# Summing the modulation columns with TensorE matmuls in four column groups instead of VectorE passes

## The chip, the cores and the metric

The kernel runs on one NeuronCore of a Trainium2 chip. The time is device microseconds of one execution; the median of several executions is compared, kernel against kernel on the same chip. The core's engines are TensorE (PE, with its weight loads shown as PEld), VectorE (DVE), ScalarE (ACT), GpSimd (POOL) and the queue of DMA issues on SyncE (SP). They run side by side and wait for each other by semaphores.

## The reference: what is computed

One inference step of a two-layer trunk on 128 context and 1,024 latent tokens, 1,152 in all, with 1,024 channels. Layer 0 mixes tokens by a bidirectional retention and a chunked gating MLP, layer 1 by a bidirectional gated linear recurrence; each is followed by a squared-ReLU MLP of width 4,096. Each sub-layer is normalized and modulated by a shift, a scale and a gate that come from a conditioning vector, one for the context and one for the latents:

```python
for l in range(DEPTH):                       # DEPTH = 2
    mod = (silu(cond) @ mod_w[l] + mod_b[l])[:, None, :]   # mod_w[l]: 1024 x 6144
    sh1, sc1, g1, sh2, sc2, g2 = jnp.split(mod, 6, axis=-1)
    h = rmsnorm(x, norm_mix[l]) * (1.0 + sc1) + sh1
    mix = token_mixing[l](h)                 # retention and gating MLP, or recurrence
    x = x + g1 * mix
    h = rmsnorm(x, norm_mlp[l]) * (1.0 + sc2) + sh2
    ff = jnp.square(jax.nn.relu(h @ mlp_w1[l])) @ mlp_w2[l]
    x = x + g2 * ff
```

The change concerns the first line: the product of two conditioning vectors (context and latents) with the modulation weights, 96 columns of 128 channels over both layers. All arithmetic is at float32 precision.

## The kernel before

**Layout.** Activations lie with channels on the 128 partitions and the 1,152 tokens along them, in eight tiles `x[:, k, :]`. A projection of 1,024 inputs to 128 outputs is a *unit*: `project` calls `three_passes` (the matmuls of L800), eight tiles by three products (high by high, high by low, low by high parts of input and weight) by three banks of 384 tokens, 72 matmuls. Results go to one of two sets of three PSUM banks, taken in turn by `take_set`; the reader gives a set back by `read_out`. GpSimd splits each unit's weights into high and low parts (L689, L691), SyncE loads them two units ahead (`load_unit`, L519).

**Stages.** First, tokens are turned into columns, and the scale and shift columns of layer 0 are made (16 of the 96) with whole rows of `mod_w` as the moving operand: `row_half` (L896) holds 32 conditioning columns `cond_wide` (two real, 30 zero) as weights in four column groups of the array and streams 512 columns of weights past each, and `first_columns` (L903) turns the sums back into columns. Then layer 0: four *heads*, each with six units and ten small stages (*minis*: transposes with `turn`, L832, and 128x128 products) interleaved in an order written out by hand; `out_proj`; the first MLP, eight *groups* of four units in and four units out (`mlp`). Then layer 1 and its MLP, which have no modulation columns to make. Each engine has a program of its own, with loops of the same shape (`head`, `group`).

**Modulation columns before.** The other 80 columns are made one at a time, eight in each head and six in each group of the first MLP, in the background of the work that they are for. SyncE's `load_mod` (L521 to L527) brings the 1,024 x 128 weights of a column in two halves to `mod_raw`, a single buffer: a half is loaded once the sum of the column before has read it (`mod_summed`). VectorE's `sum_mod` (L1724 to L1750) multiplies the eight 128x128 tiles by the conditioning value of their row and adds them up, for the two conditioning vectors, 16 passes in two dependent chains (L1734, L1739), into `mod_sum`. TensorE's `mod_column` (L821 to L828) then sums over the partitions: two matmuls with `mod_sum` as weights and one column of ones (L827) into `mod_psum`. `mods_out` (L1721) adds the bias and puts a batch of columns into `mod`, from which later steps take shifts, scales and gates.

**Order around it.** In a head TensorE's order is unit 0, the column left over from the head before, unit 1, column 0, a mini, unit 2, column 1, and so on (`mod_col`). VectorE does the sum of column n between the same stages (`next_mod`), and SyncE issues column m behind the weights of a unit as `mods_behind` says. In the MLP, columns follow the units (`mod_col(j - 1)`, `mod_col(3)`, `mod_col(2 + j)`). In the first head the rope tables, the first column, weights and the two cached states are issued one after another on SyncE, while ScalarE issues a spill of all of x to memory (`spill`, L1493).

Of the kernel before, what the change touches and what calls it, by code (L numbers as in the profile page):

```python
# [33 lines left out]
P = 128  # L34
# [137 lines left out]
def build(nc, a):  # L172
    with ExitStack() as ctx:
# [31 lines left out]
        mod_sum = sb("mod_sum", [2, 2, P])  # L205
# [78 lines left out]
        row_sum = sb("row_sum", [NCH])  # L284
        mod = sb("mod", [2, MODS, 2])
# [21 lines left out]
        mod_psum = banks[:, 2 * BANKS, 512 - 4 * MODS:512]  # L307
        ssq_psum = banks[:, 2 * BANKS + 1, :]
# [19 lines left out]
        mod_summed = sem("mod_summed")  # L328
        mod_used = sem("mod_used")
# [451 lines left out]
        def _(pe):  # L781
# [39 lines left out]
            def mod_column(i, per, c):  # L821

                pe.wait_ge(mod_summed, at(i, 2 * per, 2 * (c - FIRST_MODS) + 4))
                start = at(i, 2 * per, 2 * c)
                for n in range(2):
                    dst = mod_psum[:, start + n:start + n + 1] if isinstance(start, int) else mod_psum[:, ds(start + n, 1)]
                    last = pe.matmul(dst, mod_sum[:, c % 2, n, :], ones[:, 0:1], start=True, stop=True)  # L827
                last.then_inc(mod_used, 1)  # L828
# [97 lines left out]
            def head(h):  # L926
# [37 lines left out]
                def mod_col(c):  # L964
                    if c == 0:
                        pe.wait_ge(mod_read, h + FIRST_BATCHES)
                    mod_column(h, HEAD_MODS, M0 + c)

                big(0, 0).then_inc(unit_done, 1)
                if not first_head(h):  # L970
                    mod_column(h, HEAD_MODS, M0 - 1)
                big(1, 1).then_inc(unit_done, 1)
                mod_col(0)
# [4 lines left out]
                mod_col(1)  # L978
# [3 lines left out]
                mod_col(2)  # L982
                big(5, 3).then_inc(unit_done, 1)
                mod_col(3)
# [12 lines left out]
                last.then_inc(mini_done, 1)  # L997
                big(9, 4).then_inc(unit_done, 1)
                mod_col(4)
# [12 lines left out]
                mod_col(5)  # L1012
# [4 lines left out]
                mod_col(6)  # L1017
# [35 lines left out]
            def mlp(l):  # L1053
                I, U = AT_MLP[l].items, AT_MLP[l].units

                def group(g):
                    def mod_col(c):
                        if l == 0:
                            if c == 0:
                                pe.wait_ge(mod_read, g + (FIRST_BATCHES + HEADS))  # L1060
                            mod_column(g, GRP_MODS, MODS + c)
# [581 lines left out]
        def _(dve):  # L1643
# [28 lines left out]
            dve.tensor_copy(ident[:], consts[:, C_ID:C_ID + P])  # L1672
            dve.tensor_copy(q_rows[:].rearrange("p d t -> p (d t)"), consts[:, C_QF:C_QF + 2 * P])
# [50 lines left out]
            def sum_mod(i, per, c):  # L1724

                dve.wait_ge(mod_used, at(i, per, c - 1))
                for half in range(2):
                    dve.wait_ge(mod_landed[half], at(i, 16 * per, 16 * (c - FIRST_MODS + 1)))
                    for k in range(KT // 2):
                        for n in range(2):  # L1730
                            w, total = mod_raw[:, half, k, :], mod_sum[:, c % 2, n, :]
                            s = cond[:, n, half * KT // 2 + k:half * KT // 2 + k + 1]
                            if half + k == 0:
                                op = dve.tensor_scalar(total, w, s, None, ALU.mult)  # L1734
                                op.then_inc(dve_step, 1)
                                done = steps.done()
                            else:
                                after(chain[n])
                                op = dve.scalar_tensor_tensor(out=total, in0=w, scalar=s, in1=total, op0=ALU.mult, op1=ALU.add)  # L1739
                                if k == KT // 2 - 1 and n == 1:  # L1740
                                    op.then_inc(mod_summed, 1)
                                    done = None
                                else:
                                    op.then_inc(dve_step, 1)
                                    done = steps.done()
                            chain[n] = done
                    if half == 0:

                        dve.wait_ge(mod_summed, at(i, 2 * per, 2 * (c - FIRST_MODS) + 3))
                        chain[1] = chain[0]  # L1750

            chain = [None, None]
# [82 lines left out]
            def mlp(l):  # L1835
# [3 lines left out]
                def group(g, last):  # L1839
                    if l == 0:  # L1840
                        steps.enter(None if last else g, 14 * GRP_MODS)
                    for j in range(GRP):
# [19 lines left out]
                        if l == 0:  # L1862
                            sum_mod(g, GRP_MODS, MODS + j)
                    for k in range(2 * GRP):
                        s = (I + GRP + k) % 2
                        if k % 2 == 0:
                            dve.wait_ge(mini_done, at(g, GRP_MINIS, M + k // 2 + 1))
                        else:
                            dve.wait_ge(unit_done, at(g, GRP_UNITS, U + GRP + k // 2 + 1))
                        update(s, k, l, G2).then_inc(read_out[s], 1)  # L1870
                        if l == 0 and k in (1, 3):
                            sum_mod(g, GRP_MODS, MODS + GRP + k // 2)
                        if last and k and l == 0:
                            low_part(k - 1, gained(norm, k - 1)[:], H_NORM[norm], k - 1)
                        if last and k > 1:
                            add_square(norm, k - 1)
                        if last and k == 0 and l == 0:
                            gains_early()
                    if l == 0:
                        steps.leave(1 if last else GROUPS - 1)  # L1880
                        mods_out(1, g * GRP_MODS, GRP_MODS, at(g, GRP_MODS, MODS + GRP_MODS))
# [193 lines left out]
            def head(h, last_head):  # L2075
                steps.enter(None if isinstance(h, int) else h, 41 + 14 * HEAD_MODS)
# [7 lines left out]
                def next_mod(n):  # L2084
                    sum_mod(h, HEAD_MODS, FIRST_MODS + n)
# [31 lines left out]
                scale_out(s, 1, v_raw).then_inc(read_out[s], 1)  # L2117
                mini(0)
# [5 lines left out]
                next_mod(1)  # L2124
                next_mod(2)
# [4 lines left out]
                next_mod(3)  # L2130
# [10 lines left out]
                scale_out(s, 3, v_raw).then_inc(read_out[s], 1)  # L2141
                mini(2)
# [271 lines left out]
```

## Time and profile before

| | |
|---|---|
| Median of 3 runs | 2621.42 us (2617.94 to 2622.23) |
| The profiled execution | 2624.58 us, span 2622.4 us |
| TensorE busy | 2534.9 us, 97% of the span |
| VectorE busy | 1791.2 us, 68% |
| ScalarE / GpSimd busy | 803.9 us / 794.3 us |
| Mean DMA rate | 73 GB/s |
| Modulation sums on VectorE (L1734, L1739) | 160 and 1,120 instructions, 82.8 and 337.6 us |
| Column matmuls on TensorE (L827) | 320 records, 41.0 us |

Busy times are sums of what an engine was at work on; matmuls are pipelined, so that neighbours overlap, and a matmul's recorded duration is longer than the time until the next one starts. The stages lie at these times of the span: first columns to 65 us, the four heads from there to 469 us, the output projection to 562 us, the first MLP with its norm to some 1,403 us, layer 1 behind it.

### The profile page before, as it was taken

Reading aid. Unit: us, or ns where it says so; the run is one execution under the profiler, and the core shown is the slowest. Engines: PE = TensorE matmul, PEld = TensorE weight load, DVE = VectorE, ACT = ScalarE, POOL = GpSimd, SP = SyncE. Lnnn points to the kernel's source line nnn. Section 1 sums busy time; section 2 is a strip of 40 time slices with the busy share of each in tenths; the row PEclk is TensorE's granted clock in tenths of the full one; section 3 lists DMA queues with packets and bytes.
Section 4 is the critical chain, followed back from the end, with each engine's and each line's share of the span. In section 5 each row is a group of like instructions: output and inputs, shape, how many; then the busy total and the mean of one; then the engine's idle time right before and its main releaser. Section 6 shows DMA issues by size and latency. Waiting matters only on the chain.

```text
span 2622.4 us, 42028 instructions
## 1 busy us (share of the span) xinstructions
PE 2534.9 (97%) x15122; PEld 2476.8 (94%) x15122; DVE 1791.2 (68%) x3174; ACT 803.9 (31%) x1271; POOL 794.3 (30%) x575
## 2 busy tenths in 40 slices
PE   8999999999999999999999999799999999999998
PEld 6999999899999999999998888598999999999987
DVE  5888778568567576585588988836756556656664
ACT  5333223132102112011035666703323432432323
POOL 1221221322222222222222221122445445535521
PEclk8999999999999999999999999899999999999999
DMA  6422222312222222222222111222111011111131
GB/s 247 157 74 75 73 76 67 129 49 81 65 73 72 64 78 66 64 88 60 76 80 102 39 40 40 63 78 96 50 48 48 32 48 48 40 40 56 32 121 73
DMA packets 261367, 190.71 MB, mean 73 GB/s; under 512 B 9253, under 2 KB 253733, under 8 KB 260262
## 3 DMA queue, kind: packets, MB, share of 16 engines
q1 hardware_dynamic: 260004, 174.71, 21.8%
q10 hardware_dynamic: 1282, 14.93, 1.4%
q8 instruction: 50, 0.82, 0.1%
q14 instruction: 31, 0.25, 0.0%
HBM read 170.20 MB, written 19.41 MB: 72 GB/s over the span
## 4 chain that ended last, share of the span: by engine, by line
PE 78%; DVE 14%; issue 4%; ACT 2%; DMA 1%; SPq 0%; DVEq 0%; POOL 0%; ACTq 0%; POOLq 0%
PE psum L800 61%; PE psum L1131 12%; DVE mod_sum L1739 2%; PE psum L1182 2%; DVE gated_f L2308 1%; PE psum L827 1%; DVE h_lo L1772 1%; DVE sumsq L1710 1%; DVE x L1796 1%; DMA mod_raw<-in_mod_w 1%; DVE sumsq L1781 1%; DVE h_lo L1765 1%; DMA x_spill<-x 1%; DVE x L1968 0%; DVE mod_sum L1734 0%
## 5 line engine op out<-in xcount | busy, mean ns | idle before, releaser
L800 PE MATMUL psum<-h_hi,w_hi 128*128 128x384 f32 (+1 forms) x2880 | 674.1, 342 | 23.2 <-DVE gate_raw L1791 9.5
L800 PE MATMUL psum<-h_lo,w_hi 128*128 128x384 f32 (+1 forms) x2880 | 660.6, 338 | 0.0
L800 PE MATMUL psum<-h_hi,w_lo 128*128 128x384 f32 (+1 forms) x2880 | 660.0, 337 | 0.0
L800 PEld LDWEIGHTS psum<-h_hi,w_hi 128*128 128x128 f32 x2880 | 514.8, 189 | 36.9 <-issue 9.9
L689 POOL CAST w_hi<-w_raw 128x1024 fp32r<-128x1024 f32 x120 | 132.9, 1108 | 1321.6 <-PE psum L800 786.1
L800 PEld LDWEIGHTS psum<-h_lo,w_hi 128*128 128x128 f32 x2880 | 519.7, 189 | 0.0
L800 PEld LDWEIGHTS psum<-h_hi,w_lo 128*128 128x128 f32 x2880 | 518.3, 189 | 0.0
L1739 DVE SCALAR_TENSOR_TENSOR mod_sum<-mod_raw,cond,mod_sum 128x128 f32<-128x128 f32 x1120 | 337.6, 371 | 9.8 <-DMA mod_raw<-in_mod_w 2.2
L1796 DVE SCALAR_TENSOR_TENSOR x<-psum,mod,x 128x768 f32<-128x768 f32 (+2 forms) x264 | 145.9, 611 | 244.3 <-PE psum L800 244.3
L691 POOL TENSOR_TENSOR w_lo<-w_raw,w_hi 128x1024 fp32r<-128x1024 f32 x120 | 289.5, 2412 | 9.6
L1955 DVE TENSOR_TENSOR x<-x,psum 128x576 f32<-128x576 f32 x280 | 203.7, 752 | 103.1 <-PE psum L1131 102.5
L1319 ACT ACTIVATE relu<-relu,bias 128x384 f32<-128x384 f32 x64 | 36.0, 609 | 612.3 <-DVE relu L1851 612.3
L800 PE MATMUL psum<-hid_hi,w_hi 128*128 128x384 f32 x864 | 199.6, 338 | 7.3 <-DVE raw L1906 6.3
L800 PE MATMUL psum<-hid_lo,w_hi 128*128 128x384 f32 x864 | 196.7, 335 | 0.0
L800 PE MATMUL psum<-hid_hi,w_lo 128*128 128x384 f32 x864 | 196.5, 335 | 0.0
L1131 PE MATMUL psum<-b_hi,w_hi 128*128 128x288 f32 x784 | 168.1, 296 | 2.9 <-DVE raw L1906 2.0
L1131 PE MATMUL psum<-b_lo,w_hi 128*128 128x288 f32 x784 | 167.9, 296 | 0.0
L1131 PE MATMUL psum<-b_hi,w_lo 128*128 128x288 f32 x784 | 167.9, 296 | 0.0
L800 PEld LDWEIGHTS psum<-hid_hi,w_hi 128*128 128x128 f32 x864 | 153.1, 189 | 8.4 <-DVE raw L1906 6.6
L800 PEld LDWEIGHTS psum<-hid_lo,w_hi 128*128 128x128 f32 x864 | 154.7, 188 | 0.0
L800 PEld LDWEIGHTS psum<-hid_hi,w_lo 128*128 128x128 f32 x864 | 154.4, 188 | 0.0
L1131 PEld LDWEIGHTS psum<-b_hi,w_hi 128*128 128x128 f32 x784 | 126.6, 189 | 3.3 <-DVE raw L1906 2.2
(279 smaller groups left out, 3090.3 us busy)
## 6 DMA issues: line engine op xcount, KB each, us to landing
w_raw<-in_mlp_w SPq DMA_DIRECT2D x128, 512.0 KB, 4.1
mod_raw<-in_mod_w SPq DMA_DIRECT2D x160, 256.0 KB, 2.9
x_spill<-x ACTq DMA_DIRECT2D x3, 4608.0 KB, 14.5
w_raw<-in_ab_w_in SPq DMA_DIRECT2D x24, 512.0 KB, 4.3
w_raw<-in_lru_w_in SPq DMA_DIRECT2D x16, 512.0 KB, 4.2
x<-x_spill SPq DMA_DIRECT2D x2, 2880.0 KB, 9.6
x_old<-x_spill SPq DMA_DIRECT2D x8, 576.0 KB, 6.3
x_rows<-in_x_sample SPq DMA_DIRECT2D x8, 512.0 KB, 6.8
```

The lines of the kernel that those rows point to most:

```text
L689: pool.tensor_copy(w_hi[:, s, :], w_raw[:, s, :]).then_inc(hi_done, 1)
L691: pool.tensor_tensor(w_lo[:, s, :], w_raw[:, s, :], w_hi[:, s, :].bitcast(F32), ALU.subtract).then_inc(split_done, 1)
L800: mm = pe.matmul(psum[:, s, c, 0:end - c * CH], w, v[:, k, c * CH:end], start=(first and n == 0 and w is hi[k] and v is in_hi), stop=(last ...
L827: last = pe.matmul(dst, mod_sum[:, c % 2, n, :], ones[:, 0:1], start=True, stop=True)
L1131: mm = pe.matmul(banks[:, pair + b, 0:HB], w, v[:, p, hb, b * HB:(b + 1) * HB], start=(p == 0 and m == 0), stop=(p == 1 and m == 2))
L1182: last_mm = pe.matmul(psum[:, s, c, 0:CH], gate_w[:, 2 * d + kind, :], xc[:, c * CH:(c + 1) * CH], start=True, stop=True)
L1319: act.activation(relu[:, t], relu[:, t], ACT.Relu, bias=bias[:, j, 0:1]).then_inc(relu_ready, 1)
L1710: dve.tensor_tensor(sumsq[:], sumsq[:], square(n, k)[:], ALU.add).then_inc(sq_added, 1)
L1739: op = dve.scalar_tensor_tensor(out=total, in0=w, scalar=s, in1=total, op0=ALU.mult, op1=ALU.add)
L1765: dve.tensor_tensor(h_lo[:, k, 0:width], of, h_hi[:, k, 0:width].bitcast(F32), ALU.subtract).then_inc(h_ready, 1)
L1796: last = dve.scalar_tensor_tensor(out=dst, in0=src, scalar=mod[:, l, gate + k, c:c + 1], in1=dst, op0=ALU.mult, op1=ALU.add)
L1955: last = dve.tensor_tensor(t, t, banks[:, pair:pair + 2, 0:HB], op)
```

## The change

The sum over the 1,024 rows is made by TensorE alone, in the way the first 16 columns are made, 128 columns at a time. `mod_burst` waits for a half of `mod_raw` and does four matmuls, one in each column group, with the conditioning columns of a tile (`cond_wide`, 128x32) as weights and the 128x128 tile of `mod_raw` as moving operand; the second half adds to the same sums in `row_psum`, a part of the bank that holds `mod_psum`. VectorE's `row_out` copies the 128x128 result to `mod_row`. `mod_column` does one matmul with `mod_row` as weights and `pick` (two columns that pick and add the four groups' rows of each conditioning vector) as moving operand, and gives both values of the column. The 16 VectorE passes and their chains go away. A half of `mod_raw` is now free when TensorE's burst has read it (`mod_summed` comes from TensorE).

Column and burst stand together (`mods`): behind a unit, TensorE does the matmul of the column before and then the burst of the next. The column that stood between a mini and unit 3, and the one behind unit 3, move to other places, as do VectorE's `next_mod` calls. DMA issues stay as they are.

```diff
             def mod_column(i, per, c):
 
-                pe.wait_ge(mod_summed, at(i, 2 * per, 2 * (c - FIRST_MODS) + 4))
+                pe.wait_ge(row_copied, at(i, per, c - FIRST_MODS + 1))
                 start = at(i, 2 * per, 2 * c)
-                for n in range(2):
-                    dst = mod_psum[:, start + n:start + n + 1] if isinstance(start, int) else mod_psum[:, ds(start + n, 1)]
-                    last = pe.matmul(dst, mod_sum[:, c % 2, n, :], ones[:, 0:1], start=True, stop=True)
-                last.then_inc(mod_used, 1)
+                dst = mod_psum[:, start:start + 2] if isinstance(start, int) else mod_psum[:, ds(start, 2)]
+                pe.matmul(dst, mod_row[:, c % 2, 0, :], pick[:], start=True, stop=True).then_inc(mod_used, 1)
+
+            def mod_burst(i, per, c):
+
+                for half in range(2):
+                    pe.wait_ge(mod_landed[half], at(i, 16 * per, 16 * (c - FIRST_MODS + 1)))
+                    for q in range(KT // 2):
+                        last = pe.matmul(row_psum[WIDE * q:WIDE * (q + 1), :], cond_wide[:, half * KT // 2 + q, :], mod_raw[:, half, q, :],
+                                         start=(half == 0), stop=(half == 1))
+                    last.then_inc(mod_summed, 1)
...
-                def mod_col(c):
-                    if c == 0:
+                def mods(column, burst):
+
+                    if column == 0:
                         pe.wait_ge(mod_read, h + FIRST_BATCHES)
-                    mod_column(h, HEAD_MODS, M0 + c)
+                    if column >= 0 or not first_head(h):
+                        mod_column(h, HEAD_MODS, M0 + column)
+                    mod_burst(h, HEAD_MODS, M0 + burst)
 
                 big(0, 0).then_inc(unit_done, 1)
-                if not first_head(h):
-                    mod_column(h, HEAD_MODS, M0 - 1)
+                mods(-1, 0)
                 big(1, 1).then_inc(unit_done, 1)
-                mod_col(0)
+                mods(0, 1)
...
                 big(3, 2).then_inc(unit_done, 1)
-                mod_col(1)
+                mods(1, 2)
                 s = mini(4)
                 pe.wait_ge(activated, at(h, HEAD_UNITS, 2))
                 turn(s, v_raw).then_inc(mini_done, 1)
-                mod_col(2)
                 big(5, 3).then_inc(unit_done, 1)
-                mod_col(3)
+                mods(2, 3)
...
+                mods(3, 4)
                 big(9, 4).then_inc(unit_done, 1)
-                mod_col(4)
+                mods(4, 5)
...
-                mod_col(5)
+                mods(5, 6)
...
                 big(13, 5, heads_passed if isinstance(h, int) and h == HEADS - 1 else None).then_inc(unit_done, 1)
-                mod_col(6)
+                mods(6, 7)
...
                         project(g, GRP_ITEMS, I + j, GRP_UNITS, U + j, *waits).then_inc(unit_done, 1)
-                        if j:
-                            mod_col(j - 1)
+                        mods(j - 1, j)
...
-                    mod_col(3)
+                    mods(3, 4)
...
                         if j > 1:
-                            mod_col(2 + j)
+                            mods(2 + j, 3 + j)
...
-            def sum_mod(i, per, c):
-
+            def row_out(i, per, c):
+
+                dve.wait_ge(mod_summed, at(i, 2 * per, 2 * (c - FIRST_MODS) + 4))
                 dve.wait_ge(mod_used, at(i, per, c - 1))
...
+                dve.tensor_copy(mod_row[:, c % 2, 0, :], row_psum).then_inc(row_copied, 1)
```

In VectorE's program `next_mod` and the MLP's `sum_mod` call `row_out`; in a head the copies of columns 1, 2 and 3 stand behind the scaling of units 1, 2 and 3.

## Rows read from the trace of the kernel before

**Rows 1.** The page: its chain by engine, and one of the costliest groups.

```profile
PE 78%; DVE 14%; issue 4%; ACT 2%; DMA 1%; SPq 0%; DVEq 0%; POOL 0%; ACTq 0%; POOLq 0%
...
L1739 DVE SCALAR_TENSOR_TENSOR mod_sum<-mod_raw,cond,mod_sum 128x128 f32<-128x128 f32 x1120 | 337.6, 371 | 9.8 <-DMA mod_raw<-in_mod_w 2.2
```

**Rows 2.** Windows: stretch and its length, busy us of each engine, clock, DMA.

```profile
core 0: us, PE busy (x) PEld busy (x) DVE busy (x) ACT busy (x) POOL busy (x), PEclk, DMA share, GB/s
706.00:1324.00 618.00, 618.00 (x3604) 617.89 (x3602) 402.62 (x966) 78.75 (x168) 165.15 (x96) 1.00 0.24 71
```

**Rows 3.** Timeline of TensorE in the first MLP: start, duration, instructions merged.

```profile
641.90 0.50 PE L827 MATMUL psum<-ones,mod_sum 128*128 128x1 f32 x4
642.26 0.79 PE L800 MATMUL psum<-hid_hi,w_hi 128*128 128x384 f32 x3
642.89 0.68 PE L800 MATMUL psum<-hid_lo,w_hi 128*128 128x384 f32 x3
```

**Rows 4.** Timeline around the shift rows, matmuls in four column groups.

```profile
51.51 0.69 PE L800 MATMUL psum<-h_hi,w_lo 128*128 128x384 f32 x3
52.12 0.16 PEld L896 LDWEIGHTS psum<-shift_raw,cond_wide 128*32 128x32 f32 x8 [0.25 <-issue]
52.12 3.64 PE L896 MATMUL psum<-shift_raw,cond_wide 128*32 128x512 f32 x32
52.58 0.13 PEld L896 LDWEIGHTS psum<-shift_raw,cond_wide 128*32 128x32 f32 x4 [0.30 <-issue]
53.01 0.13 PEld L896 LDWEIGHTS psum<-shift_raw,cond_wide 128*32 128x32 f32 x4 [0.30 <-issue]
...
55.70 0.80 PE L800 MATMUL psum<-h_hi,w_hi 128*128 128x384 f32 x3
...
56.33 0.68 PE L800 MATMUL psum<-h_lo,w_hi 128*128 128x384 f32 x3
```

**Rows 5.** The chain that ended last: start, us on the chain, what.

```profile
214.05 2.13 PE psum L987 x18
...
667.83 12.59 PE psum L800 x72
```

**Rows 6.** Waits of TensorE: waiting line, releaser, us in all, times, longest.

```profile
PE psum L827 <- DVE mod_sum L1739: 7.4, 8, 2.0
...
PE psum L800 <- DVE probs L2212: 1.3, 1, 1.3
...
PE psum L800 <- DVE x L1796: 1.0, 3, 0.4
```

**Rows 7.** Timeline of TensorE, first and last head; idle before in brackets.

```profile
97.71 0.81 PE L800 MATMUL psum<-h_hi,w_hi 128*128 128x384 f32 x3 [0.73 <-DVE turned L1791]
...
111.95 0.50 PE L827 MATMUL psum<-ones,mod_sum 128*128 128x1 f32 x4
...
465.84 3.19 PE L1024 MATMUL psum<-wsT,kT 128*128 128x128 f32 x18 [3.49 <-DVE k_fwd L1791]
```

**Rows 8.** Windows of 2 us behind two idle times; PEclk before DMA share.

```profile
98.00:100.00 2.00, 2.00 (x9) 2.00 (x9) 2.00 (x3) 1.97 (x3) 1.67 (x1) 0.59 1.04 311
...
468.00:470.00 2.00, 2.00 (x9) 2.00 (x9) 2.00 (x1) 1.44 (x2) 2.00 (x1) 0.50 0.00 0
```

**Rows 9.** Timeline of TensorE: the first matmuls of unit 1, first head.

```profile
65.29 0.98 PE L800 MATMUL psum<-h_hi,w_hi 128*128 128x384 f32 x3
```

**Rows 10.** Line L527 in two stretches: issues, first and last; landing.

```profile
L527 SPq DMA_DIRECT2D mod_raw<-in_mod_w x2: 378/410/441, 61.4 to 61.8; - x2
...
DMA to landing us min/median/max: 5.4/5.9/6.3
...
L527 SPq DMA_DIRECT2D mod_raw<-in_mod_w x2: 379/379/379, 69.9 to 75.2; - x2
...
DMA to landing us min/median/max: 9.2/11.4/13.7
```

**Rows 11.** DMA issues from 55 to 100 us: KB, median us to landing.

```profile
x_spill<-x ACTq DMA_DIRECT2D x1, 4608.0 KB, 16.9
```

More of the change, by code:

```diff
@@ L204, in build @@
         mod_raw = sb("mod_raw", [2, KT // 2, P], mod_raw_at)
-        mod_sum = sb("mod_sum", [2, 2, P])
+        mod_row = sb("mod_row", [2, 2, P])
         t_at = [region(TB) for _ in range(10)]
@@ L284, in build @@
         row_sum = sb("row_sum", [NCH])
+        pick = sb("pick", [2])
         mod = sb("mod", [2, MODS, 2])
@@ L307, in build @@
         mod_psum = banks[:, 2 * BANKS, 512 - 4 * MODS:512]
+        row_psum = banks[:, 2 * BANKS, 0:P]
         ssq_psum = banks[:, 2 * BANKS + 1, :]
@@ L328, in build @@
         mod_summed = sem("mod_summed")
+        row_copied = sem("row_copied")
         mod_used = sem("mod_used")
@@ L1056, in group, with mods @@
                 def group(g):
-                    def mod_col(c):
+                    def mods(column, burst):
                         if l == 0:
-                            if c == 0:
+                            if burst == 0:
                                 pe.wait_ge(mod_read, g + (FIRST_BATCHES + HEADS))
-                            mod_column(g, GRP_MODS, MODS + c)
+                            if column >= 0:
+                                mod_column(g, GRP_MODS, MODS + column)
+                            if burst < GRP_MODS:
+                                mod_burst(g, GRP_MODS, MODS + burst)
                     for j in range(GRP):
@@ L1672, in _ @@
             dve.tensor_copy(ident[:], consts[:, C_ID:C_ID + P])
+            dve.tensor_copy(pick[:], consts[:, C_SEL:C_SEL + 2])
             dve.tensor_copy(q_rows[:].rearrange("p d t -> p (d t)"), consts[:, C_QF:C_QF + 2 * P])
@@ L1722, in mods_out @@
                                   ALU.add).then_inc(mod_read, 1)
-            def sum_mod(i, per, c):
+            def row_out(i, per, c):
+                dve.wait_ge(mod_summed, at(i, 2 * per, 2 * (c - FIRST_MODS) + 4))
                 dve.wait_ge(mod_used, at(i, per, c - 1))
[L1727 to L1752, printed above, removed]
+                dve.tensor_copy(mod_row[:, c % 2, 0, :], row_psum).then_inc(row_copied, 1)
             def gains(n, batches):
@@ L1839, in group @@
                 def group(g, last):
-                    if l == 0:
-                        steps.enter(None if last else g, 14 * GRP_MODS)
                     for j in range(GRP):
@@ L1862, in group @@
                         if l == 0:
-                            sum_mod(g, GRP_MODS, MODS + j)
+                            row_out(g, GRP_MODS, MODS + j)
                     for k in range(2 * GRP):
@@ L1870, in group @@
                         update(s, k, l, G2).then_inc(read_out[s], 1)
-                        if l == 0 and k in (1, 3):
-                            sum_mod(g, GRP_MODS, MODS + GRP + k // 2)
+                        if l == 0 and k in (1, 5):
+                            row_out(g, GRP_MODS, MODS + GRP + k // 4)
                         if last and k and l == 0:
@@ L1879, in group @@
                     if l == 0:
-                        steps.leave(1 if last else GROUPS - 1)
                         mods_out(1, g * GRP_MODS, GRP_MODS, at(g, GRP_MODS, MODS + GRP_MODS))
@@ L2075, in head @@
             def head(h, last_head):
-                steps.enter(None if isinstance(h, int) else h, 41 + 14 * HEAD_MODS)
+                steps.enter(None if isinstance(h, int) else h, 41)
                 def unit(n):
@@ L2084, in next_mod @@
                 def next_mod(n):
-                    sum_mod(h, HEAD_MODS, FIRST_MODS + n)
+                    row_out(h, HEAD_MODS, FIRST_MODS + n)
                 def rotate(dst):
@@ L2117, in head @@
                 scale_out(s, 1, v_raw).then_inc(read_out[s], 1)
+                next_mod(1)
                 mini(0)
@@ L2123, in head @@
                 dve.tensor_scalar(by_bank(k_bwd[:]), whole(s), col(k_dec[:, 1, :], h), None, ALU.mult).then_inc(read_out[s], 1)
-                next_mod(1)
-                next_mod(2)
                 unit(2)
@@ L2129, in head @@
                 scale_out(s, 2, turned).then_inc(read_out[s], 1)
-                next_mod(3)
+                next_mod(2)
                 dve.wait_ge(projected, h * 2 + 2)
@@ L2141, in head @@
                 scale_out(s, 3, v_raw).then_inc(read_out[s], 1)
+                next_mod(3)
                 mini(2)
```

## The prediction

> **What bounds the kernel now.** I read the page first, then the windows by stage, then TensorE's timeline at the places that the diff touches, then its waits, and last the DMA rows of the first head. On the page the chain that ended last is TensorE for 78% and VectorE for 14%, and VectorE's largest removed group is 1,120 instructions of the modulation sums, 337.6 us [rows 1]. That looks like a large prize. The windows correct it: in six of the eight groups of the first MLP TensorE is busy for 618.00 of 618.00 us, while VectorE is busy for 402.62 [rows 2]. So in most of the stretch with modulation columns VectorE's time is hidden behind TensorE, and the profiled execution is 2622.4 us of span with 2.2 us around it. What the change takes off VectorE counts only where TensorE waits; what it gives TensorE counts nearly everywhere. The waits of TensorE on the sums are 7.4 us in 8 places [rows 6].
>
> **The columns on TensorE, old and new.** There are 80 columns: 4 heads of 8 and 8 groups of 6. A column now is two matmuls, four records. In the MLP they hold TensorE from 641.90 to 642.26, 0.36 us, and the next three matmuls take 0.63 us (642.26 to 642.89) [rows 3] where three of 72 in 12.59 us take 0.52 [rows 5]: 0.10 more, so a column costs 0.46 us. The new column is one matmul of the same shape with two columns instead of one. It should leave two records of 0.09 us, 0.18 us in all (below: it can't go under one record, 0.09; above: it costs what two do, 0.36).
>
> **The burst.** Each column gets eight new matmuls, two in each of four column groups, 128 columns long. Their like stands in the trace before: the shift rows, 16 matmuls of 512 columns on the same conditioning weights in the same four groups, 32 records [rows 4]. Their weight loads come in fours, at 52.58 and 53.01: a round of four takes 0.43 us, so four groups do run side by side. A quarter of the columns should take a quarter of that, 0.107 us, and a lone 128-column record in another place takes 2.13/18 = 0.118 [rows 5]. A burst is two matmuls deep, two records each: four rounds, 0.43 us. But the shift rows hold TensorE longer than their rounds. The three matmuls before would have ended at 51.51 + 0.52 = 52.03; the next begin at 55.70 and take 0.63 to 56.33, 0.11 too long. From 52.03 to 55.81 is 3.78 us, eight rounds are 3.41, so going into column groups and out again costs 0.37 [rows 4]. A burst is then 0.80 us.
> The Trainium skill (TensorEngine Tiling, Key Properties) says that changing the tiling mode drains TensorE. Every burst would pay that twice; the trace agrees, with 0.37 us for both, and a sum that left it out would be 80 x 0.37 = 30 us lower.
> Net per column: 0.18 + 0.80 - 0.46 = +0.52 us, 80 times is **+41.6 us**. It lies on the path wherever TensorE has no gap, which is all of the MLP. Below: no switch, +0.15 each, 12 us. Above: nothing side by side and each record at the 0.09 of today's short ones, 16 x 0.09 + 0.37 + 0.18 - 0.46 = +1.53, 122 us. I take the value of the shift rows, the same kind of matmul.
>
> **What VectorE gives back.** The waits on the sums, 7.4 us [rows 6], end: a copy of 128x128 in place of 16 passes of 371 ns [rows 1] is behind the burst by much less than the unit that follows. Their places are columns 2 and 5 of the first head, 5 and 6 of the later ones and one in the first MLP. Behind column 2 of the first head comes a wait of 0.73 us for the scaled unit, late because the sums stood ahead of it, and then unit 3 takes 97.71 to 111.95 = 14.24 us instead of 12.59 [rows 5, 7]: the granted clock, which had been full, is 0.59 in a stretch of 2 us after these two idle times, so mostly at 1.2 GHz, the lower of its two levels [rows 8]. That is 0.73 + 1.65. In the last head the last unit's scaling on VectorE stands behind the sums: TensorE idles 3.49 us, its next 18 records take 3.19 instead of 2.13 [rows 5, 7], and in the 2 us after that the clock is 0.50, that is 1.2 GHz, which costs another 1.0 [rows 8]. Then it waits 1.3 us for the masked sums `probs`, behind column 7's sum [rows 6]. Together 6.9. At the end of the MLP, waits of 1.0 us on the update of x stand behind two sums [rows 6]; I count them all. Sum: 7.4 + 2.4 + 6.9 + 1.0 = **-17.7 us**. Below: only the 7.4. Above: 20, with some short waits on other buffers that the bursts cover. The 80 copies cost nothing on the path: VectorE is idle for a third of the MLP [rows 2]. Uncovered they would be at most a pass each, 80 x 0.37 = 30 us.
>
> **What is late next.** The burst waits for the weights on TensorE itself, where before VectorE waited and TensorE went on. Behind the waiting instruction stand the next projection and so all later units. In the first head this bites twice. Unit 1 starts at 65.29 now [rows 9]. In the new order burst 0 stands before it, and column 0's halves are issued at 61.4 and 61.8 and land 5.4 and 6.3 us later, the second at 68.1 [rows 10]. That is 2.8 us of idle, less little: 2.7. Then column 1's load can go only after burst 0. Now it is issued at 69.9 and 75.2 and lands 13.7 and 9.2 us later, at 83.6 and 84.4 [rows 10], because it shares the engines with the 4.6 MB spill of x, 16.9 us [rows 11]. It will be issued some 3 us sooner but lie in the same queue behind that spill, so I take the same landing. TensorE ends unit 1 at about 68.6 + 12.6 = 81.2 and wants it then: 2.7 us once the burst's own time is taken off. I charge each stall one lowering of the clock, as behind the two idle times above, 1.6 us. Sum **+8.6 us**; below 2.7 (column 1 lands sooner, no lowering), above 12.
> From column 2 on a load goes when the burst before has read, and has a 12.6 us unit until the next. Bursts 4 and 6 of a head are closer, with only the short stages between (some 7 us), against 5.4 to 6.3 for a load even in the first head's traffic [rows 10]: nothing. SP's later loads stand behind these; they wait for TensorE instead of VectorE and go no later, so projection weights stay early.
>
> **Rivals.** (A) The forecast: 41.6 + 8.6 - 17.7 = +32.5 us. (B) It doesn't get slower: the switch of groups hides under the neighbours, so a column's net is +0.15 and the bill 12 us against 17.7 given back. For it: the chain gives VectorE 14% [rows 1]. Against it: the 0.37 is there in the only burst of this kind. It gives 2621 + 12 + 3 - 18 to 2621 + 12 + 9 - 18, that is 2618 to 2624; it decides if burst and column together take about 0.6 us (today's 0.46 and 0.15), where A has 0.98. (C) Short records don't run side by side: each is bound by its own start, 0.09 us as in today's columns [rows 3], and the bill is 122 us: 2621 + 122 + 9 - 18 = 2734. Against it: the eight first weight loads of the shift rows come within 0.16 us [rows 4].
> The Trainium skill (TensorEngine Tiling, Instruction Overhead) gives each matmul about 60 cycles; at 2.4 GHz that is 25 ns, an estimate, and 16 of them 0.40 us a burst: 32 us more if it adds up, nothing if the groups' streams cover it. The shift rows are too long to show it.
> (D) Loads come late in every head, not the first alone: bursts 4 and 6 wait. If such a load took the 9.2 us of the busy stretch [rows 10] it would be 2 to 3 us late, 8 times, 16 to 24 us: about 2674. Against it: no such traffic after the first head.
>
> **How the numbers follow.** A 0.74, B 0.12, C 0.07, D 0.07. The profiled execution, 2624.6 us, lies 3.2 above the median of the three timed runs; from the median, 2621.4 + 32.5 = 2654. A's own bounds: a switch dearer or cheaper by a third (80 x 0.12 = 10 us), stalls 3 to 12, gains 10 to 20 give 2636 to 2676. The range reaches on to 2630 and 2684, which takes D in and leaves out C and most of B. Within 0.2% is about what a measurement of this kernel can tell from no change, 5 us. A, C and D are slower; half of B is within, a little of it faster: faster 0.05, same 0.07, slower 0.88.
>
> **What would show it.** In the MLP: the group of eight units grows from 103.0 us by 6 x 0.52 = 3.1; bursts of 16 records over about 0.4 us and a gap of 0.2 to 0.3 us behind them. If the gap is missing, B; if a burst spans 1.4 us or more, C. In the first head: TensorE idle on a load of the modulation weights near 65 and 81 us. In later heads: no wait on modulation at all (else D). In the last head: no idle ahead of the group mixing, and no lowered clock. The forecast is wrong if a burst's whole price is not between 0.6 and 1.0 us.

## The result, and the profile after

The changed kernel takes **2641.5 us** (median of 4 runs, 2638.5 to 2642.4) against 2621.8 for the kernel before on the same chip (4 runs, 2617.9 to 2625.9). The ratio is 1.0073, 95% interval 1.0055 to 1.0090: some 20 us slower, where 32.5 were forecast. The profiled executions have spans of 2639.0 us after and 2622.4 before, 16.6 us apart.

On the page, the busy shares and the chain by engine answer to [rows 1]:

```profile
PE 2562.5 (97%) x16242; PEld 2488.4 (94%) x16242; DVE 1406.7 (53%) x1975; ACT 803.9 (30%) x1271; POOL 793.1 (30%) x575
...
PE 84%; DVE 8%; issue 3%; ACT 2%; DMA 1%; SPq 0%; DVEq 0%; POOL 0%; ACTq 0%; POOLq 0%
```

VectorE's share of the chain fell from 14% to 8%, and TensorE's rose from 78% to 84%. The window over the six groups of the first MLP in which TensorE never rests answers to [rows 2]:

```profile
core 0: us, PE busy (x) PEld busy (x) DVE busy (x) ACT busy (x) POOL busy (x), PEclk, DMA share, GB/s
640.31:1274.75 634.44, 634.44 (x4105) 625.31 (x4105) 238.67 (x427) 78.67 (x168) 164.88 (x97) 1.00 0.24 70
```

VectorE has some 160 us less to do here and nothing is gained by it: six groups that took 618.00 us, from the second line of [rows 3] at 642.26 to the same place six groups later in the timeline of before, now take 634.44, at the same full clock:

```profile
1260.27 0.78 PE L800 MATMUL psum<-hid_hi,w_hi 128*128 128x384 f32 x3
```

The timeline of TensorE shows one column and burst, against [rows 3]:

```profile
704.36 0.68 PE L803 MATMUL psum<-h_hi,w_lo 128*128 128x384 f32 x3
704.88 0.28 PE L829 MATMUL psum<-pick,mod_row 128*128 128x2 f32 x2
705.08 0.65 PE L836 MATMUL psum<-mod_raw,cond_wide 128*32 128x128 f32 x16
705.66 0.79 PE L803 MATMUL psum<-h_hi,w_hi 128*128 128x384 f32 x3
706.28 0.69 PE L803 MATMUL psum<-h_lo,w_hi 128*128 128x384 f32 x3
```

From 704.88 to 705.66 is 0.78 us, where the old column had 0.36, and the three matmuls behind take 0.62, 0.10 too long, as they did before. In place of [rows 6], the waits of TensorE name no modulation sum any more, and only 1.0 us for the loads:

```profile
PE psum L1007 <- DVE s_bwd L2136: 3.7, 4, 0.9
...
PE psum L836 <- DMA mod_raw<-in_mod_w: 1.0, 2, 0.6
```

The end of the last head, against the last line of [rows 7] and of [rows 8] (timeline, and a window of 2 us):

```profile
464.59 2.17 PE L1036 MATMUL psum<-wsT,kT 128*128 128x128 f32 x18
467.29 0.79 PE L803 MATMUL psum<-h_hi,w_hi 128*128 128x384 f32 x3 [0.53 <-ACT mix L1570]
```

```profile
468.00:470.00 2.00, 2.00 (x14) 2.00 (x13) 1.56 (x2) 0.87 (x2) 1.86 (x2) 1.00 0.00 0
```

The idle 3.49 us ahead of the group mixing is gone, its 18 records take 2.17 us and not 3.19, and the granted clock is 1.00.

**Where the 16.6 us lie**, from the starts of the same matmuls in both timelines: the stretch before the shift rows, which the change doesn't touch, is 2.3 us shorter (49.81 against 52.12); from the shift rows to the second projection of the MLP's first group, 577.0 us against 577.2, which is all of the heads, the output projection and the first four bursts and three columns of the MLP; from there to the gates of layer 1, which is the rest of the MLP, 820.8 against 801.8, so +19.0; behind it +0.1. The heads gave back about what their bursts cost, and the MLP carries the bill. Behind the gates of layer 1, where no run changes anything, the profiles of all eleven kernels lie between 1187.9 and 1196.6 us; so what a change is worth is read below from the stages that it touches.

### The profile page after: what moved, and what is told of

Same layout as the page of the kernel before. It is cut to its first block, busy times and chain, and to the rows that moved or that the text cites. A ratio compares the mean times of both kernels' runs of the same rounds, so it can differ in the third digit from the quotient of the medians.

```text
span 2639.0 us, 42175 instructions
## 1 busy us (share of the span) xinstructions
PE 2562.5 (97%) x16242; PEld 2488.4 (94%) x16242; DVE 1406.7 (53%) x1975; ACT 803.9 (30%) x1271; POOL 793.1 (30%) x575
## 4 chain that ended last, share of the span: by engine, by line
PE 84%; DVE 8%; issue 3%; ACT 2%; DMA 1%; SPq 0%; DVEq 0%; POOL 0%; ACTq 0%; POOLq 0%
PE psum L803 65%; PE psum L1145 12%; PE psum L1196 2%; PE psum L836 2%; DVE gated_f L2296 1%; DVE h_lo L1763 1%; PE psum L842 1%; DMA mod_raw<-in_mod_w 1%; DMA x_spill<-x 1%; DVE x L1956 0%; DVE sumsq L1725 0%; DVE s_bwd L2136 0%; PE psum L1007 0%; DVE b_lo L1911 0%; PE psum L998 0%
```

## The experiments

Each ratio is to the kernel before on the same chip, with its 95% interval. The profiles' periods are those between the first matmuls of the second projection (`hid_hi`) in consecutive groups of the first MLP, 6 columns each: 102.99 us before, 105.74 after; those of a head lie between the first matmuls of its last product (`wsT`).

**1. The sums left out of the kernel before.**

```diff
 for half in range(2):
     dve.wait_ge(mod_landed[half], ...)
-    for k in range(KT // 2):
-        for n in range(2):
...
-                op = dve.scalar_tensor_tensor(out=total, in0=w, scalar=s, in1=total, op0=ALU.mult, op1=ALU.add)
...
+    dve.sem_inc(passed, 1)
+    dve.nop().then_inc(mod_summed, 1)
```

> The kernel before with VectorE's sums left out; its waits for the weights, its semaphores and all of TensorE's columns stay. It leaves out the sums of the modulation columns (zeros stand in their place). This is what the change gives back, by itself. Theory (the give-back is TensorE's waits on the sums and what stands behind them): 12 to 18 us faster than before, 2604 to 2610, and the idle time ahead of the group mixing in the last head is gone. Rival (VectorE's share of the chain, 14%, is a prize of its own, and the added work ate it): 30 us faster or more, below 2592. Rival (VectorE's sums were hidden all along): within 5 us of before.

2612.8 us, ratio 0.9954 (0.9941 to 0.9968): 11 to 12 us faster, just short of the theory's 12 to 18 and outside both rivals. The groups of the MLP keep their 102.99 us. The four heads, up to the second projection, fall from 577.2 to 562.8 us: 5.9 in the first, 1.4 and 1.1 in the next two, 4.8 in the last, 1.3 behind it. From the last group's second projection to the gates of layer 1 the profile falls from 80.9 to 79.7 us. So nearly all that VectorE can give back is in the heads, 14.5 us of the profile. TensorE's wait for `s_bwd` (the states of the backward pass, which VectorE makes) stays as it was before, which matters for run 2:

```profile
PE psum L997 <- DVE s_bwd L2129: 3.7, 4, 0.9
```

**2. The bursts left out of the changed kernel.**

```diff
-    for q in range(KT // 2):
-        last = pe.matmul(row_psum[...], cond_wide[...], mod_raw[...], ...)
-    last.then_inc(mod_summed, 1)
+    pe.sem_inc(passed, 1)
+    pe.nop().then_inc(mod_summed, 1)
...
-    dve.tensor_copy(mod_row[:, c % 2, 0, :], row_psum)
+    dve.tensor_copy(mod_row[:, c % 2, 0, :], ones[:])
```

> The changed kernel with the eight matmuls of every burst left out; the waits of TensorE on the weights, the copies on VectorE and the new one-matmul columns stay. It leaves out the sums of the modulation columns (ones stand in their place). Theory (the added time is the bursts' occupation of TensorE): without them the kernel falls by 80 x 0.55 to 0.68 us, 44 to 54, minus what the bursts cover in the heads: 2590 to 2602, so 20 to 30 us faster than before. Rival (the added time is TensorE waiting for the weights): it stays within 10 us of the changed kernel, 2632 or more.

2612.3 us, ratio 0.9955 (0.9940 to 0.9971): 29 us below the changed kernel, outside both expectations. The MLP does what the theory says: a group takes 101.93 us, 3.81 less than with bursts, 0.635 for each. The heads don't: from the shift rows to the second projection the profile is only 2.3 us shorter than the changed kernel's. TensorE waits 9.1 us for `s_bwd` where the changed kernel has 3.7, and it has short waits on VectorE that the changed kernel doesn't have, of which the second row is one:

```profile
PE psum L1005 <- DVE s_bwd L2134: 9.1, 4, 2.3
PE psum L803 <- DVE turned L1780: 1.6, 4, 0.4
```

The durations of VectorE's write into `mod_row`, minimum, median and maximum, here and then in the changed kernel, point to the cause of the long wait (view of one line: count, nanoseconds, first and last start):

```profile
L1741 DVE COPY mod_row<-ones x80: 208/224/2404, 68.7 to 1378.1; 128x128 f32<-128x128 f32 x80
```

```profile
L1743 DVE COPY mod_row<-psum x80: 273/278/293, 68.6 to 1407.3; 128x128 f32<-128x128 f32 x80
```

The timeline of VectorE and that of GpSimd in the run, at one of the long ones:

```profile
185.79 2.39 DVE L1741 COPY mod_row<-ones 128x128 f32<-128x128 f32 x1
...
185.69 2.40 POOL L694 TENSOR_TENSOR w_lo<-w_raw,w_hi 128x1024 fp32r<-128x1024 f32 x1
```

Where the copy meets GpSimd's subtraction it ends with it, at 188.2 and 188.1 us. So it goes with the other long ones, 23 of the 32 copies in the heads: each ends with a GpSimd instruction. One of them stands right ahead of VectorE's work on `s_bwd` in each head, as here in head 1 (heads are counted from 0):

```profile
214.66 2.34 DVE L1741 COPY mod_row<-ones 128x128 f32<-128x128 f32 x1
216.92 0.28 DVE L2131 COPY s_bwd<-psum 128x128 f32<-128x128 f32 x1
```

The copy out of the accumulator (PSUM) is never held up so. So this run has a fault of its own, which runs 8 and 9 go after; the short waits are those that a burst covers in the changed kernel (see the heads, below).

**3 and 4. The change in the heads alone, and in the MLP alone.**

Both against the changed kernel: heads only (`mod_col` calls the `mod_column` of before), then MLP only:

```diff
-mods(j - 1, j)
+if j:
+    mod_col(j - 1)
...
-row_out(g, GRP_MODS, MODS + j)
+sum_mod(g, GRP_MODS, MODS + j)
```

```diff
-mods(0, 1)
+mod_col(0)
...
-row_out(h, HEAD_MODS, FIRST_MODS + n)
+sum_mod(h, HEAD_MODS, FIRST_MODS + n)
...
+dve.nop().then_inc(row_copied, 32)
```

> Bursts and new columns in the four heads, VectorE's sums and old columns in the first MLP. Theory (in the heads the bursts pay about what the removed waits give; the MLP carries the bill): 2617 to 2622, 0 to 5 us faster than before. Rival (the first head's late weights carry the bill): 2630 or more. Rival (a burst costs the same everywhere, 0.46 net, and the heads give back 12 to 15 us): 2620 to 2625.

> VectorE's sums and old columns in the four heads, bursts and new columns in the first MLP. Theory (48 columns at a net of 0.46 us on a TensorE that has no gap): 20 to 22 us slower than before, 2641 to 2644, as slow as the whole change. Rival (the bill is in the first head): within 8 us of before.

Heads only: 2619.2 us, ratio 0.9982 (0.9974 to 0.9991), 5 us faster than before. MLP only: 2642.1 us, ratio 1.0072 (1.0060 to 1.0084), as slow as the whole change, with groups of 105.74 us. Both as the theory had it: the place is the MLP. Run 3's third expectation, the same price for a burst everywhere, began at 2620, too near to be told by the median; the heads' periods speak against it (1.8 us for eight bursts, below, where 0.46 each would be 3.7).

Run 3 also shows the loads that the prediction was afraid of. Its timeline of TensorE in the first head, and the window behind the first wait:

```profile
67.07 0.43 PE L846 MATMUL psum<-mod_raw,cond_wide 128*32 128x128 f32 x8 [1.11 <-DMA mod_raw<-in_mod_w]
67.97 0.66 PE L846 MATMUL psum<-mod_raw,cond_wide 128*32 128x128 f32 x8 [0.47 <-DMA mod_raw<-in_mod_w]
68.56 1.33 PE L804 MATMUL psum<-h_hi,w_hi 128*128 128x384 f32 x3
...
83.22 0.42 PE L846 MATMUL psum<-mod_raw,cond_wide 128*32 128x128 f32 x8 [0.50 <-DMA mod_raw<-in_mod_w]
84.09 0.43 PE L846 MATMUL psum<-mod_raw,cond_wide 128*32 128x128 f32 x8 [0.45 <-DMA mod_raw<-in_mod_w]
```

```profile
68.00:70.00 2.00, 2.00 (x12) 1.62 (x13) 0.36 (x2) 1.87 (x3) 0.08 (x1) 0.50 1.38 451
```

Both waits stand where they were put, near 67 and 83 us, but take 1.58 and 0.95 us; behind the first the granted clock is 0.50 (1.2 GHz), behind the second it is 1.00.

**5. Twice the stream in each burst.**

```diff
+if half == 0:
+    for q in range(KT):
+        pe.matmul(banks[WIDE * (q % 4):WIDE * (q % 4 + 1), 2 * BANKS, P:2 * P],
+                  cond_wide[:, q, :], mod_raw[:, 0, q % 4, :], start=True, stop=True)
 for q in range(KT // 2):
     last = pe.matmul(row_psum[...], cond_wide[...], mod_raw[...], ...)
```

> The changed kernel with eight more matmuls in every burst, of the same kind and into the same four column groups, two per group, into columns of the bank that nothing reads; no more changes into or out of column groups. Theory (four more rounds of records at 0.107 us each, the size that the shift rows gave): a group of eight units in the MLP goes from 105.74 to 108.3 us (6 x 0.43), the kernel about 34 us slower than the changed one, 2674 to 2678. Rival (the price of a burst is mostly going into and out of column groups, and the records run closer than that): a group of 106.6 or less, the kernel under 12 us slower, 2653 or less. Rival (each record is bound by its own start of 0.09 us): a group of 114.4, the kernel 115 us slower.

2671.3 us, ratio 1.0181 (1.0162 to 1.0199), 28 to 30 us above the changed kernel, a little under the theory's 34 and far from both rivals; a group of the MLP takes 108.34 us. That is 2.60 for six bursts, **0.433 us** for four rounds (a round is one record in each of the four groups): the 0.43 that the prediction took from the shift rows. The timeline of TensorE:

```profile
706.10 0.65 PE L837 MATMUL psum<-mod_raw,cond_wide 128*32 128x128 f32 x16
706.56 0.62 PE L840 MATMUL psum<-mod_raw,cond_wide 128*32 128x128 f32 x16
707.11 0.79 PE L803 MATMUL psum<-h_hi,w_hi 128*128 128x384 f32 x3
```

The second sixteen records begin 0.46 us behind the first. In heads 1 and 2 the period grows by 3.0 us for eight bursts, 0.37 each: there too the path is TensorE's, with a little slack.

**6. The same matmuls over the whole width, without column groups.**

```diff
-pe.matmul(row_psum[WIDE * q:WIDE * (q + 1), :], cond_wide[:, ...], mod_raw[:, half, q, :],
-          start=(half == 0), stop=(half == 1))
+pe.matmul(row_psum, cond_full[:, ...], mod_raw[:, half, q, :],
+          start=(half == 0 and q == 0), stop=(half == 1 and q == KT // 2 - 1))
```

> The changed kernel with conditioning weights of all 128 columns (zero but for two), so that the eight matmuls of a burst add up in one group over the whole width: no column groups, no change into or out of them, the same number of records. Theory (four groups run side by side; without them sixteen records of 0.11 to 0.12 us follow each other, and the 0.2 to 0.3 us for the groups' change falls away): a burst of 1.8 to 1.9 us in place of 0.635, a group of the MLP at 112.7 to 113.4, the kernel 90 to 105 us slower than the changed one, 2731 to 2746. Rival (column groups don't run side by side): a group of 104 to 105.7, the kernel as the changed one or up to 20 us faster.

2726.5 us, ratio 1.0392 (1.0370 to 1.0414), 85 us above the changed kernel, a little under the theory's bounds; a group takes 112.39 us, so a burst (112.39 - 101.93) / 6 = 1.74 us, sixteen records of 0.109:

```profile
704.64 0.28 PE L831 MATMUL psum<-pick,mod_row 128*128 128x2 f32 x2
704.78 2.03 PE L838 MATMUL psum<-mod_raw,cond_full 128*128 128x128 f32 x16
706.56 0.77 PE L805 MATMUL psum<-hid_hi,w_hi 128*128 128x384 f32 x3
```

With column groups sixteen records take 0.433 (run 5), a quarter. The four groups run side by side, and the rival that they don't falls.

**7. The change in the last head alone.**

```diff
+if not (isinstance(h, int) and h == HEADS - 1):
+    head_sums(h, big, mini)
+    return
...
 mods(-1, 0)
...
+dve.nop().then_inc(row_copied, 24)
```

`head_sums` is a head in the order of before; the MLP is that of before as well.

> Bursts and new columns in the last head alone; the first three heads and the MLP keep VectorE's sums and the old columns. Theory (in the last head alone the sums stand ahead of work that TensorE waits for; the removed idle time, 3.5 and 1.3 us and what the lowered clock costs behind it, is worth more than eight bursts): 4 to 6 us faster than before, 2616 to 2620, faster than both kernels and no slower than with bursts in all heads. Rival (all heads pay alike): 1 us faster than before.

2616.0 us, ratio **0.9969** (0.9957 to 0.9981), 5 to 11 us faster than before. It has the lowest median of the versions that compute all columns, though its interval overlaps that of run 3. In its profile the last head and what follows it to the second projection take 264.7 us against 268.8 before, 4.05 less; the rest of what the medians show isn't found in stages that the edit touches.

**8. Without bursts again, VectorE writing a product.**

```diff
-dve.tensor_copy(mod_row[:, c % 2, 0, :], ones[:])
+dve.tensor_tensor(mod_row[:, c % 2, 0, :], ones[:], ones[:], ALU.mult)
```

> The changed kernel without the bursts, as in the run without bursts above, but what VectorE writes into the rows is a product of two tiles and not a copy of one: there the copy took 1791 ns on average, and one that began at 185.79 ended at 188.18, with GpSimd's subtraction of 185.69 to 188.09. It leaves out the sums of the modulation columns. Theory (VectorE's copy stood behind GpSimd's instructions and held up the heads; the bursts' price is hidden by that): the product takes 0.2 to 0.4 us, TensorE's longer waits on s_bwd are gone, and the kernel comes to 2598 to 2606, 36 to 44 us below the changed kernel. Rival (TensorE's waits for the weights hold the heads): it stays at 2610 to 2614.

2611.9 us, ratio 0.9957 (0.9942 to 0.9973): the repair did nothing, and the wait on `s_bwd` is 9.5 us. The time lies within the rival's bounds, but VectorE's durations show that the product stands behind GpSimd as the copy did, so the run doesn't speak for TensorE's waits on the loads:

```profile
L1741 DVE TENSOR_TENSOR mod_row<-ones x80: 275/287/2469, 68.4 to 1379.5; 128x128 f32<-128x128 f32 x80
```

**9. Two matmuls over the whole width in place of a burst.**

```diff
-for q in range(KT // 2):
-    last = pe.matmul(row_psum[WIDE * q:WIDE * (q + 1), :], cond_wide[...], mod_raw[:, half, q, :], ...)
+last = pe.matmul(row_psum, ident[:], mod_raw[:, half, 0, :], start=(half == 0), stop=(half == 1))
```

> The changed kernel with each burst cut to two matmuls over all 128 columns, one for each half of the weights, without column groups; VectorE copies the result out of the accumulator as in the changed kernel. It leaves out the sums over the other six blocks of rows. It asks two things. What does the change of groups cost: the four records take as long as the four rounds of a burst, 4 x 0.107 us, but nothing goes into or out of column groups; by theory (0.20 us of a burst's 0.635 is that change) a group of the MLP takes 101.93 + 6 x 0.43 = 104.5 us against 105.74, by the rival (the change costs nothing, the sixteen records cost it) 103.3 or less, by the other (0.37, as the shift rows gave) the gap would be 2.2 and the group 103.5 with more than 0.43 in the records. And what held up the heads without bursts: if it was VectorE's write standing behind GpSimd, it takes 0.28 us again here, the wait on s_bwd is 0.93 and not 2.3, and head 1 is shorter than the changed kernel's 102.68 us, at 101 to 102; if it was something else in a head without bursts, the wait of 2.3 stays. The kernel by theory: 2626 to 2631.

2626.8 us, ratio 1.0004 (0.9994 to 1.0015). The wait on `s_bwd` is back to 3.7 us:

```profile
PE psum L1005 <- DVE s_bwd L2134: 3.7, 4, 0.9
```

Run 1, which has neither bursts nor copies, has the same 3.7, so the long wait of run 2 came from what VectorE wrote from SBUF, not from the missing bursts. Head 1 takes 102.06 us, as much as in run 2 (102.02): what the waits give back, the four records take. A group of the MLP takes 104.35 us, and the four records (104.35 - 101.93) / 6 = 0.403 us:

```profile
699.66 0.28 PE L829 MATMUL psum<-pick,mod_row 128*128 128x2 f32 x2
699.80 0.69 PE L835 MATMUL psum<-mod_raw,ident 128*128 128x128 f32 x4
700.25 0.77 PE L803 MATMUL psum<-h_hi,w_hi 128*128 128x384 f32 x3
```

The groups' change thus costs (105.74 - 104.35) / 6 = 0.23 us by this run, and 0.635 - 0.433 = 0.20 by runs 2 and 5; neither the rival of nothing nor 0.37 fits. The periods can be read from these first matmuls of consecutive groups, of runs 2, 9, the changed kernel, 5 and 6 in this order:

```profile
726.61 0.77 PE L803 MATMUL psum<-hid_hi,w_hi 128*128 128x384 f32 x3
...
828.54 0.77 PE L803 MATMUL psum<-hid_hi,w_hi 128*128 128x384 f32 x3
```

```profile
726.78 0.77 PE L803 MATMUL psum<-hid_hi,w_hi 128*128 128x384 f32 x3
...
831.12 0.77 PE L803 MATMUL psum<-hid_hi,w_hi 128*128 128x384 f32 x3
```

```profile
732.59 0.79 PE L803 MATMUL psum<-hid_hi,w_hi 128*128 128x384 f32 x3
...
838.33 0.79 PE L803 MATMUL psum<-hid_hi,w_hi 128*128 128x384 f32 x3
```

```profile
748.81 0.79 PE L803 MATMUL psum<-hid_hi,w_hi 128*128 128x384 f32 x3
...
857.15 0.79 PE L803 MATMUL psum<-hid_hi,w_hi 128*128 128x384 f32 x3
```

```profile
777.45 0.77 PE L805 MATMUL psum<-hid_hi,w_hi 128*128 128x384 f32 x3
...
889.84 0.77 PE L805 MATMUL psum<-hid_hi,w_hi 128*128 128x384 f32 x3
```

## Why the prediction was right, and which terms were off

**The direction and the mechanism were right.** The sums on VectorE were hidden behind TensorE in the MLP (run 1: not a tenth of a microsecond of a group's period), the bursts are not (run 4). The result lies in the range, at 0.6 of the forecast loss. Most of the miss is in the heads. For the MLP the forecast was 48 x 0.52 - 1.0 = 24.0 us; the profile has 19.0 and some 1.8 for the four bursts ahead (an estimate, 4 x 0.458). For the heads it was 8.5, and the profile shows about nothing. Three terms of the bill were too big, and the gain in the heads was a little too big as well, which hid part of it.

**The burst.** Column and burst were to take 0.98 us and take 0.46 + 2.75 / 6 = 0.92, so the net per column in the MLP is 0.458 and not 0.52. That is a mean over a group: where column and burst stand together they hold TensorE for 0.78 and 0.10 behind them, as the timeline above shows, and the first burst and the last column of a group stand apart, so that there the 0.10 is paid once more. By parts: the new column 0.28 (0.46 less (102.99 - 101.93) / 6), the stream 0.433, the change of groups 0.20 to 0.23. The prediction had 0.18, 0.43 and 0.37; it counted the 0.10 us behind a burst in the last, so 0.27 is what compares with the 0.20 to 0.23, and 0.28 with the new column. (Eight rounds of the 0.43 that it read are 3.44 us and not 3.41, so the shift rows give 0.34 rather than 0.37.) The step "going into column groups and out again costs 0.37", read off the one place with shift rows, is the one that was mis-sized, by some 0.05 us, which is 4 us over 80 columns. A burst's price, 0.635 us, lies just inside the 0.6 to 1.0 that the prediction set as its test. The Trainium skill (TensorEngine Tiling, Key Properties) says that a change of tiling mode drains TensorE; runs 2, 5 and 9 agree, with a price of 0.20 to 0.23 us for going in and out. The Trainium skill (TensorEngine Tiling, Instruction Overhead) gives a matmul about 60 cycles, for sixteen records an estimate of 0.40 us. Here that doesn't add to the stream: by run 5 sixteen records take 0.433 us in all, a quarter of what four rounds of the shift rows take for four times the columns (4 x 0.43).

**The heads.** They were to lose 16.6 us by bursts and 8.6 by late loads and to win 16.7; that would be 8.5 us slower. In the changed kernel's profile they are level (with four bursts of the MLP counted in), and in run 3 they are 3.3 us faster. The give-back was about right: 14.5 us by run 1. What was too dear is the other side: with bursts in place of nothing (run 3 against run 1) the heads take 11.2 us more, not 25.2.
In heads 1 and 2 eight new columns with their bursts cost 1.8 us more than the old columns and not 4.2. Each place still grows by 0.42 us, 8 x 0.42 = 3.4, but the small stages behind some of the bursts shrink: TensorE had short waits there, which now pass while the burst runs. The timeline of run 1, and then of the changed kernel, at one such place:

```profile
178.49 0.50 PE L828 MATMUL psum<-ones,mod_sum 128*128 128x1 f32 x4
178.85 1.18 PE L833 MATMUL psum<-ident,kT 128*128 128x128 f32 x9
180.24 0.79 PE L801 MATMUL psum<-h_hi,w_hi 128*128 128x384 f32 x3 [0.21 <-DVE v_raw L1772]
```

```profile
185.54 0.65 PE L836 MATMUL psum<-mod_raw,cond_wide 128*32 128x128 f32 x16
186.12 1.20 PE L842 MATMUL psum<-ident,kT 128*128 128x128 f32 x9
187.09 0.79 PE L803 MATMUL psum<-h_hi,w_hi 128*128 128x384 f32 x3
```

The transposes and what is behind them take 1.39 us there and 0.97 here, 0.42 less, of which the row shows 0.21 as idle time: a matmul's recorded end, which overlaps the next start where nothing waits, covers the rest. Four such places and two smaller ones make 1.7 us a head. The prediction named "short waits on other buffers that the bursts cover" for its upper bound of 20 us and left them out of the sum.

**The late loads.** They come where the prediction put them, at bursts 0 and 1 of the first head and nowhere else, so rival D falls. But they were to cost 2.7 us each and the clock 1.6 each; run 3 has 1.58 and 0.95, and one lowering, so about 4 us in place of 8.6 (an estimate, 1.58 + 0.95 + 1.6). In the changed kernel's own profile burst 0 didn't wait at all: the clock had fallen to 0.50 ahead of it, from about 60 us, and unit 0's end came that much later, some 5 us (an estimate: ten us, to 70, at half the clock):

```profile
60.00:62.00 2.00, 2.00 (x9) 0.50 0.78 303
62.00:64.00 2.00, 2.00 (x10) 0.50 1.01 348
```

On TensorE nothing that the change touches stands before that place; run 7, whose first head is that of before, has its low clock at 58 to 65 us, and run 4, whose heads are those of before, at 48 to 54. So such a lowering comes without the change too. Why the clock falls in one execution and not in another is open.

**The last head and the MLP's end.** The chain of idle time and lowered clock behind the sums was read rightly; run 7 takes the change there alone and keeps the gain. The end of the MLP was to give 1.0 us; from the last group's second projection to the gates it takes 80.6 us against 80.9, bursts included, and 79.7 in run 1: a gain of 1.2 where 1.0 was forecast.

**The rivals.** B needed column and burst together at 0.6 us; they take 0.92. C needed 1.4 us for a burst; it takes 0.635. Without column groups it would take 1.74 (run 6).

## What to carry to other kernels

An engine's work counts by stage: 420.4 us of sums on VectorE (82.8 + 337.6) were worth 12 us here, nearly all of it in the heads, and moving them to the engine that has no gap cost more than that in the stage where they were free. Make such a move only where the waiting is, as in run 7; and price the target engine by the period of a loop that it fills, where a tenth of a microsecond an iteration can be read.
Before charging small additions at full price in a stage with short waits, look at what stands right behind each: half of the bursts' cost in the heads passed inside waits that were there anyway.

## What the runs showed of the hardware

VectorE's copies and products of 128x128 from SBUF to SBUF (runs 2 and 8) took 0.21 to 0.29 us alone and up to 2.40 (a copy) and 2.47 us (a product) where they began behind a GpSimd subtraction: they ended 0.08 to 0.16 us behind it, so the price was the whole rest of GpSimd's instruction. The 80 copies out of the accumulator took 0.273 to 0.293 us, though 39 of them lay beside such a subtraction. The Trainium skill (GPSIMD Engine Reference, Specifications) says that GpSimd's SBUF interfaces are shared with VectorE, with contention where VectorE's instruction runs in a two-port mode or has two SBUF inputs. Run 8, whose product has two SBUF inputs, agrees; in which mode the copy of run 2 ran, no run here shows.

Going into four column groups and out again cost 0.20 to 0.23 us (runs 2, 5 and 9); sixteen records of 128 columns in four groups took a quarter of what they took at full width (0.433 us in run 5 against 1.74 in run 6).
